# The FFN norm's sums of squares: from columns of the transposed block to rows of the residual

## Chip, cores and metric

The kernel runs on one core of one Trainium2 chip. The metric is the device time of one execution in microseconds (us), as the median of several runs. The core has a matrix engine (TensorE, PE in the profile; its weight loads are PEld), VectorE (DVE), ScalarE (ACT), GpSimd (POOL) and SyncE (SP), each with its own in-order instruction stream; they meet at semaphores.

## The reference

Two transformer-like layers run one after the other on 256 tokens of width D = 2048, in float32. What matters here lies in the middle of the first:

```
h = h + nsa_mixer(rmsnorm(h, mix_norm_g), ...)        # attention, its last product is "out"
h = h + swiglu(rmsnorm(h, ffn_norm_g), ffn_w_in, ffn_w_out)
rmsnorm(x, g) = x * rsqrt(mean(x*x, axis=-1) + 1e-6) * g
```

The FFN norm needs, for each of the 256 tokens, the sum of the squares of the 2048 features of h. The factor rsqrt(...) of a token is not applied to the operand of the product with ffn_w_in, but to the product's rows afterwards.

## The kernel before

Every large product is computed in three partial products of split float32 numbers (high times high, high times low, low times high). Weights stream through a ring of four slots in chunks of 128x1024: SP loads a chunk into `raw` (L402), ACT rounds it to the high part `w_hl` (`split`, L531), DVE subtracts to get the low part (L890), and TensorE uses it in 12 products of 128x512 (L1591 to L1593 in `block_tokens`), one chunk's work. ACT and DVE prepare a chunk three chunks ahead of TensorE (`AHEAD = 3`): ACT may write the slot of chunk c as soon as TensorE has finished chunk c-4. Work that is not splitting is put by hand between the splits: a table such as `{2: out_operand(3), ...}` says what follows the split of step j, for ACT, DVE and TensorE separately.

The attention's output product has four blocks of 512 features (B_OUT to B_OUT+3). For block n

- DVE adds the product to the residual, `row_block(n)` of `h_rows`, which has tokens in partitions: two pieces of 128 tokens x 512 features (`out_block`, L1195). This raises `taken`.
- TensorE transposes the block into PSUM, `by_features`, with features in partitions (`out_by_features`, eight transposes at L1863).
- ACT makes the high operand times the gain (L554), DVE the low one (L920), which raises `x_ready`.
- ACT squares the transposed block, 128x1024, into `sq` (`out_square`, L570), which raises `sq_ready`.
- DVE adds the 1024 columns down to 256 and onto `stat` (`h_squares`, which is `add_squares`, L956 to L961), which raises `stats_ready`.

Block 3 is handled inside the first block of the up product, `up(0, True)`. Its eight chunks are numbered 0 to 7 here, and 8 to 15 are those of the value half that follows. TensorE's steps there are: after chunk 1 the transposes of block 3, after chunk 4 the call `stats(0, 2, 5)`. That waits for DVE's last addition and multiplies `stat` by ones: two 128x256 instructions (L1696) that give the sums along a row and repeat them in all partitions, and four one-column instructions (L1698) that give them once for each partition's token. DVE makes the mean plus epsilon and its reciprocal from the 258 columns (`variance`, L926 and L927), ACT takes the root (`root`, L564), and the columns `S:S+2` of `rms[:, FFN]` scale the rows of the up product in the Sigmoid (L697) and on DVE (L1237, L1243). The 256 columns in front of them are not read in the FFN.

`down_squares` and `final_squares` do the same by columns for the final norm, with `sq` again.

Of the kernel before, what the change touches and what calls it, by code (L numbers as in the profile page):

```python
# [10 lines left out]
ACT = mybir.ActivationFunctionType  # L11
# [140 lines left out]
def program(nc, d):  # L152
    ctx = ExitStack()

    def sb(name, shape, dt=F32, scope=ctx):
        return scope.enter_context(nc.sbuf_tensor(name, shape, dt))

    def sem(name):
        return ctx.enter_context(nc.semaphore(name))
# [12 lines left out]
    cross = sb("cross", [P, HT, S])  # L172
    rms = sb("rms", [P, 4, S + TT])
    rtmp = sb("rtmp", [P, S + TT])


    with ExitStack() as s1:
# [119 lines left out]
    dve_own, act_own, pool_own = sem("dve_own"), sem("act_own"), sem("pool_own")  # L297
    xh_ready, x_ready = sem("xh_ready"), sem("x_ready")
    sq_ready, stats_ready, stats_sum = sem("sq_ready"), sem("stats_ready"), sem("stats_sum")
    var_ready, rms_ready = sem("var_ready"), sem("rms_ready")  # L300
    rel_done, u_ready, u_out, bias_in = sem("rel_done"), sem("u_ready"), sem("u_out"), sem("bias_in")
    gates_sig, gates_done, gates_ready = sem("gates_sig"), sem("gates_done"), sem("gates_ready")
# [216 lines left out]
    def _(act):  # L519
# [20 lines left out]
        def splits(at, count, extras=None, unit=None, the_set=0):  # L540

            for j in range(count):
                split(at, j + AHEAD)
                if unit is not None and j == count // 2:
                    take_cross(at.at(j), unit, sums(the_set)[1], cross[:, :, :])
                if extras and j in extras:
                    extras[j]()
            if unit is not None:
                take_cross(at.at(count), unit + 1, sums(the_set + 1)[1], cross[:, :, :])
# [9 lines left out]
            for f in range(FT):  # L559
                operand(bass.ds(n * FT + f, 1), gain, by_features[:, f:f + 1, :])  # L560

        def root(n, count):
            act.wait_ge(var_ready, count)
            a(rms[:, n, :], rtmp[:, :], ACT.Sqrt).then_inc(rms_ready, 1)  # L564

        def square(dst, src, free, scale=1.0):

            if free is not None:
                act.wait_ge(stats_ready, free)
            return a(dst, src, ACT.Square, scale=scale)  # L570
# [99 lines left out]
        def out_operand(n):  # L670
            block_operand(n, FFN, n + 1)

        def out_square(n):

            act.wait_ge(x_ready, KT + FT * (n + 1))
            square(sq[:, :, :], by_features, n + 1).then_inc(sq_ready, 1)

        splits(Pos(C_OUT), 2 * NB, attentions(3, ATT_SLOTS + 1))
        splits(Pos(C_OUT + 2 * NB), NB, {0: lambda: out_operand(0), 2: lambda: out_square(0), 4: lambda: out_operand(1),
                                         6: lambda: out_square(1)})  # L680
        splits(Pos(C_OUT + 3 * NB), NB, {2: lambda: out_operand(2), 4: lambda: out_square(2)})

        def up_high(i):
            act.wait_ge(ft_done, i + 1)
# [1 line left out]

        def up(i, first):
            at = Pos(C_UP, i, 2 * NB)
            splits(at, NB, {2: lambda: out_operand(3), 3: lambda: out_square(3), 6: lambda: root(FFN, 2)} if first else
                   {2: lambda: up_high(i - 1)})  # L690
            act.wait_ge(chunks_done, at.at(NB))

            act.wait_ge(taken, i * 2 + B_UP)
            if first:
                act.wait_ge(rms_ready, 2)
            for t in range(TT):
                last = a(f_a[:, t, :], up_set(0)[:, t, :], ACT.Sigmoid, scale=col(FFN, t))  # L697
            last.then_inc(up_sig, 1)
            splits(Pos(C_UP + NB, i, 2 * NB), NB)
# [7 lines left out]

        def down_squares(n):
            act.wait_ge(x_ready, 2 * KT + FT * (n + 1))
            square(sq[:, :, :], by_features, 5 + 2 * n).then_inc(sq_ready, 1)  # L710
            for f in range(FT):
                kt = n * FT + f
                last = square(f_squares[:, f, :], by_features[:, f, :], None, gains[:, FINAL, kt:kt + 1])
            last.then_inc(sq_ready, 1)
# [164 lines left out]
    def _(dve):  # L879
# [330 lines left out]
            dve.wait_ge(chunks_done, C_OUT + 14)  # L1210
            out_block(0)

        def h_squares(n):
            return lambda: add_squares(sq, 0, n + 5, n == 0)

        splits(Pos(C_OUT), 2 * NB, heads_out(3, ATT_SLOTS + 1) | {14: first_out}, softmaxes(3, ATT_SLOTS))
        out_block(1)
        splits(Pos(C_OUT + 2 * NB), NB, {1: lambda: out_operands(0), 3: h_squares(0), 5: lambda: out_operands(1), 7: h_squares(1)})
        out_block(2)
        splits(Pos(C_OUT + 3 * NB), NB, {3: lambda: out_operands(2), 5: h_squares(2)})  # L1220
        out_block(3)

        def up_low(i):
# [2 lines left out]
            tt(f_hl[:, kts, 1, :], by_features, f_hl[:, kts, 0, :].bitcast(F32), ALU.subtract).then_inc(f_ready, 1)  # L1226

        def up(i, first):
            splits(Pos(C_UP, i, 2 * NB), NB, {2: lambda: out_operands(3), 4: h_squares(3), 5: lambda: variance(2, 2)} if first else
                   {3: lambda: up_low(i - 1)})  # L1230
            if first:
                dve.wait_ge(rms_ready, 2)

            def gated():
                dve.wait_ge(up_sig, i + 1)
                for t in range(TT):
                    last = stt(f_a[:, t, :], up_set(0)[:, t, :], col(FFN, t), f_a[:, t, :], ALU.mult, ALU.mult)  # L1237
                last.then_inc(taken, 1)

            splits(Pos(C_UP + NB, i, 2 * NB), NB, {1: gated})  # L1240
            dve.wait_ge(taken, i * 2 + (B_UP + 1))
            for t in range(TT):
                last = stt(f_b[:, t, :], up_set(1)[:, t, :], col(FFN, t), f_a[:, t, :], ALU.mult, ALU.mult)  # L1243
            last.then_inc(taken, 1)
# [6 lines left out]
            block_operands(n, None, 2 * KT + n * FT)  # L1251

        def final_squares(j, first):
            return {first: lambda: add_squares(sq, 0, 9 + 2 * j, j == 0),
                    first + 1: lambda: add_squares(f_squares, 1, 10 + 2 * j, j == 0)}

        for n in range(4):
            splits(Pos(C_DOWN + n * ND), ND, {3: lambda n=n: down_operands(n - 1)} | final_squares(n - 1, 5) if n else
# [32 lines left out]
        def mlstm(i, first):  # L1291
# [4 lines left out]
            no_cross = NO_CROSS_ML + 3 * i  # L1296

            if first:
                splits(at, NB, {1: lambda: down_operands(3)} | final_squares(3, 3) | {6: lambda: variance(4, 2), 7: second_variance}, half=lambda: summed(
                    t1[:, 0:2, :], number, the_set, NO_CROSS_ML).then_inc(taken, 1))  # L1300

                summed(t1[:, 2:4, :], number + 1, the_set + 1, NO_CROSS_ML).then_inc(taken, 1)
                dve.wait_ge(taken, number + 2)
                dve.wait_ge(rms_ready, 4)
                own.link(tt(rms[:, PRE, :], rms[:, PRE, :], rms[:, FINAL, :], ALU.mult))
                tt(t1[:, :, :], t1[:, :, :], rows(PRE), ALU.mult).then_inc(first_normed, 1)
                splits(Pos(C_ML + NB), 1)
                dve.wait_ge(crossed, B_ML + 3 - NO_CROSS_ML)
                own.link(tt(g_fm[:, :], sets[(B_ML + 2) % 2][0:2 * MH, 0:S], cross[0:2 * MH, 0, :], ALU.add))
                tt(g_fm[:, :], sets[(B_ML + 2) % 2][0:2 * MH, S:2 * S], g_fm[:, :], ALU.add).then_inc(taken, 1)  # L1310
                dve.wait_ge(taken, B_ML + 3)
                tt(g_fm[:, :], g_fm[:, :], rms[0:2 * MH, PRE, 0:S], ALU.mult).then_inc(gates_normed, 1)
            else:

                splits(at, NB, {0: lambda: z_silu_tokens(i - 1), 1: lambda: ya_product(i - 1), 4: lambda: ya_low(i - 1)},
                       half=lambda: take(number, the_set, no_cross, t1[:, 0:2, :], PRE))
                take(number + 1, the_set + 1, no_cross, t1[:, 2:4, :], PRE)
# [253 lines left out]
    def _(pe):  # L1571
# [299 lines left out]
        def out_by_features(n):  # L1871
            if n == 0:
                pe.wait_ge(o_ready, HEADS)
            else:
                pe.wait_ge(x_ready, KT + FT * n)
                pe.wait_ge(sq_ready, 4 + n)
            rows_by_features(B_OUT + n, n)

        out_by_features(0)
# [5 lines left out]
        def up_by_features(i):  # L1885

            pe.wait_ge(taken, i * 2 + (B_UP + 2))
            if isinstance(i, int) and i == 0:
                pe.wait_ge(x_ready, 2 * KT)
                pe.wait_ge(sq_ready, 8)  # L1890
            else:
                pe.wait_ge(f_ready, i)
            back_by_features(f_b, ft_done)

        def up(i, first):
            await_set(i * 2 + B_UP)
            gemm_tokens(Pos(C_UP, i, 2 * NB), B_UP, ready=operand_ready(KT) if first else None,
                        steps={1: lambda: out_by_features(3), 4: lambda: stats(0, 2, 5)} if first else {1: lambda: up_by_features(i - 1)})
            await_set(i * 2 + (B_UP + 1))
            gemm_tokens(Pos(C_UP + NB, i, 2 * NB), B_UP + 1)  # L1900

# [3 lines left out]
        def down_by_features(n):  # L1905
            if n == 0:
                pe.wait_ge(f_ready, NUP)
            else:
                pe.wait_ge(x_ready, 2 * KT + FT * n)
                pe.wait_ge(sq_ready, 8 + 2 * n)  # L1910
            rows_by_features(B_DOWN + n, 4 + n)

        for n in range(4):
# [12 lines left out]
        def mlstm(i, first):  # L1926
            at, number = ml_block(i, 0)

            def norms():
                stats(0, 2, 13)  # L1930
                stats(1, 3, 13)


            gemm(at, number, ml_set(i, 0), ready=operand_ready(2 * KT) if first else None,
# [284 lines left out]
```

## Time and profile before

| | |
|---|---|
| runs | 2116.81, 2116.83, 2116.71 us, median 2116.81 |
| span of the profiled execution, first to last instruction | 2115.2 us |
| TensorE busy | 2104.1 us (99%); its weight loads 1772.3 us (84%) |
| DVE, ACT, POOL busy | 60%, 48%, 3% |
| idle time of TensorE with a named releaser | 1.5, 1.3 and 1.2 us |
| granted TensorE clock | 0.999 |

The page gives the profiled execution's span and no other time for it; the runs' median is 1.6 us above that span, which is what lies around the instructions. Busy time of TensorE counts overlapping instructions: a product is shown as 0.39 us long while the next starts 0.23 us after it, so its pace is read from starts, not from durations.

### The profile page before, as it was taken

How to read it: one execution, taken by the hardware profiler on the slowest of the kernel's cores; microseconds unless marked ns; L12 is line 12 of the kernel's file. 1: busy time of each engine (PE TensorE's matmuls, PEld its weight loads, DVE VectorE, ACT ScalarE, POOL GpSimd, SP SyncE). 2: the span in 40 equal slices, each digit the busy share in tenths (PEclk: the TensorE clock that was granted, in tenths of full speed). 3: DMA queues.
4: the chain of work that ended last, by engine and by line, in shares of the span. 5: the costliest groups of instructions: out<-in, count | busy, mean ns of one | idle time of the engine just before them, and what ended most of it. 6: DMA issues, size and time to landing. Idle time of an engine off the chain costs nothing.

```text
span 2115.2 us, 29340 instructions
## 1 busy us (share of the span) xinstructions
PE 2104.1 (99%) x10154; PEld 1772.3 (84%) x10154; DVE 1274.7 (60%) x1725; ACT 1010.9 (48%) x1330; POOL 64.1 (3%) x117
## 2 busy tenths in 40 slices
PE   9999999999999999999999999999999999999998
PEld 8888888888888888888888888888888888888887
DVE  7767665655555555545556766856857655455464
ACT  6465665454444444434444555444454454444444
POOL 1001221000000000000000000000000000000000
PEclk9999999999999999999999999999999999999999
DMA  8586334555555555555555455555555556555564
GB/s 299 187 275 227 139 131 144 185 179 190 190 192 184 190 190 191 188 192 189 189 189 193 157 179 178 189 177 185 189 175 183 176 184 195 190 189 191 195 229 149
DMA packets 109386, 398.72 MB, mean 189 GB/s; under 512 B 12437, under 2 KB 12469, under 8 KB 108915
## 3 DMA queue, kind: packets, MB, share of 16 engines
q1 hardware_dynamic: 106848, 386.97, 54.2%
q0 software_dynamic: 2304, 10.51, 1.4%
q8 instruction: 60, 0.98, 0.2%
q14 instruction: 30, 0.22, 0.0%
q10 hardware_dynamic: 144, 0.03, 0.0%
HBM read 393.00 MB, written 2.13 MB: 187 GB/s over the span
## 4 chain that ended last, share of the span: by engine, by line
PE 99%; ACT 0%; DVE 0%; DMA 0%; POOL 0%; issue 0%; DVEq 0%; SPq 0%; ACTq 0%
PE set L1593 23%; PE set L1591 23%; PE set L1592 23%; PE set L1617 13%; PE set L1625 7%; PE misc L1863 1%; PE misc L1744 1%; PE set L1715 1%; PE misc L1817 1%; PE misc L1804 1%; PE misc L1996 0%; PE set L1719 0%; PE misc L1790 0%; PE set L1675 0%; PE misc L1956 0%; PE misc L1792 0%
## 5 line engine op out<-in xcount | busy, mean ns | idle before, releaser
L890 DVE TENSOR_TENSOR w_hl<-raw,w_hl 128x1024 fp32r<-128x1024 f32 x729 | 890.8, 1224 | 745.0 <-ACT w_hl L531 743.0
L531 ACT ACTIVATE w_hl<-raw 128x1024 fp32r<-128x1024 f32 x729 | 771.0, 1059 | 970.6 <-PE set L1593 792.7
L1591 PE MATMUL set<-w_hl,x_hl 128*128 128x512 f32 x1408 | 553.5, 393 | 0.0
L1593 PE MATMUL set<-w_hl,x_hl 128*128 128x512 f32 x1408 | 548.6, 390 | 0.0
L1592 PE MATMUL set<-w_hl,x_hl 128*128 128x512 f32 x1408 | 547.9, 389 | 0.0
L1593 PEld LDWEIGHTS set<-w_hl,x_hl 128*128 128x128 f32 x1408 | 264.3, 188 | 55.5
L1592 PEld LDWEIGHTS set<-w_hl,x_hl 128*128 128x128 f32 x1408 | 264.5, 188 | 54.4
L1591 PEld LDWEIGHTS set<-w_hl,x_hl 128*128 128x128 f32 x1408 | 264.4, 188 | 54.1
L1617 PE MATMUL set<-x_hl,w_hl 128*128 128x512 f32 x1216 | 296.2, 392 | 0.0
L1617 PEld LDWEIGHTS set<-x_hl,w_hl 128*128 128x128 f32 x1216 | 222.2, 188 | 43.2 <-issue 0.7
L1625 PE MATMUL set<-x_hl,w_hl 128*128 128x256 f32 x1216 | 163.5, 284 | 0.0
L1625 PEld LDWEIGHTS set<-x_hl,w_hl 128*128 128x128 f32 x1216 | 157.4, 191 | 6.9 <-issue 0.7
L1591 PE MATMUL set<-w_hl,f_hl 128*128 128x512 f32 x352 | 137.3, 390 | 0.0
L1593 PE MATMUL set<-w_hl,f_hl 128*128 128x512 f32 x352 | 137.0, 389 | 0.0
L1592 PE MATMUL set<-w_hl,f_hl 128*128 128x512 f32 x352 | 136.9, 389 | 0.0
L1593 PEld LDWEIGHTS set<-w_hl,f_hl 128*128 128x128 f32 x352 | 66.1, 188 | 13.8
L1592 PEld LDWEIGHTS set<-w_hl,f_hl 128*128 128x128 f32 x352 | 66.1, 188 | 13.6
L1591 PEld LDWEIGHTS set<-w_hl,f_hl 128*128 128x128 f32 x352 | 66.1, 188 | 13.6
L1591 PE MATMUL set<-w_hl,o_hl 128*128 128x512 f32 x128 | 51.0, 399 | 0.0
L1593 PE MATMUL set<-w_hl,o_hl 128*128 128x512 f32 x128 | 50.0, 391 | 0.0
L1592 PE MATMUL set<-w_hl,o_hl 128*128 128x512 f32 x128 | 49.9, 390 | 0.0
L1591 PE MATMUL set<-w_hl,ya_hl 128*128 128x512 f32 x128 | 49.8, 389 | 0.0
(319 smaller groups left out, 1741.2 us busy)
## 6 DMA issues: line engine op xcount, KB each, us to landing
raw<-in_weights SPq DMA_DIRECT2D x730, 512.0 KB, 3.3
bias_g<-bias POOLq DMA_DIRECT2D x4, 572.0 KB, 3.4
h<-in_x SPq DMA_DIRECT2D x4, 512.0 KB, 7.0
bias<-u_dram POOLq DMA_DIRECT2D x1, 2048.0 KB, 13.6
h<-in_x_rows POOLq DMA_DIRECT2D x1, 2048.0 KB, 10.2
out<-y_t SPq DMA_DIRECT2D x8, 256.0 KB, 2.0
cur<-in_cur POOLq DMA_DIRECT2D x4, 285.0 KB, 3.7
gain_row<-in_final POOLq DMA_DIRECT2D x1, 1024.0 KB, 5.8
```

Source lines behind the costliest of these rows:

```text
L531: a(high, whole, ACT.Copy).then_inc(hi_ready, 1)
L890: tt(low, whole, high.bitcast(F32), ALU.subtract).then_inc(lo_ready, 1)
L1591: mm(o, hl[:, kt, 0, x], w[:, 0, c], start=first and k == 0, stop=False, skip_group_check=True)
L1592: mm(o, hl[:, kt, 0, x], w[:, 1, c], start=False, stop=False, skip_group_check=True)
L1593: last = mm(o, hl[:, kt, 1, x], w[:, 0, c], start=False, stop=True, skip_group_check=True)
L1617: last = mm(out[:, f * 2 * S:(f + 1) * 2 * S], w[:, 0, c], hl[:, kt, :, :], start=first and k == 0, stop=low_first, skip_group_check=True)
L1625: last = mm(out[:, f * 2 * S + S:(f + 1) * 2 * S], w[:, 1, c], hl[:, kt, 0, :], start=False, stop=not low_first, skip_group_check=True)
L1715: mm(out[:, f * 2 * S:(f + 1) * 2 * S], w[:, 0, c], x_hl[:, kt, :, :], start=kt == 0, stop=False, skip_group_check=True)
L1744: last = mm(out, blk_hl[:, n, kt, :], w[:, :, k * CH:(k + 1) * CH], start=kt == 0, stop=kt == CB - 1, skip_group_check=True)
L1804: tr(m[b][:, k * P:(k + 1) * P], pr[:, o + k * P:o + (k + 1) * P], ident[:, :])
L1817: mm(m[1][:, 0:S], v_g[:, b, 0, :], prob_t[:, b, 0:S], start=b == 0, stop=False)
L1863: last = nc.tensor.transpose(by_features[:, f, t * P:(t + 1) * P], src[:, t, f * P:(f + 1) * P], ident[:, :])
```

## The change

For the FFN norm alone, ACT takes the squares of block n from the residual's rows: two instructions over 128 tokens x 512 features, each with an accumulator output that holds one sum per token. The four blocks' sums stand in `ffn_sq`, 128x2x4. DVE adds the four, makes the mean plus epsilon and the reciprocal on two columns; ACT takes the root of two columns. DVE's four `h_squares`, TensorE's `stats` call of this norm and TensorE's waits for `sq_ready` before transposes go away, and the numbers of the semaphores that the final norm uses are shifted. The squares stay at the same places of ACT's order.

```diff
+    ffn_sq = sb("ffn_sq", [P, TT, 4])
-        def root(n, count):
+        def root(n, count, cols=slice(0, S + TT)):
             act.wait_ge(var_ready, count)
-            a(rms[:, n, :], rtmp[:, :], ACT.Sqrt).then_inc(rms_ready, 1)
+            a(rms[:, n, cols], rtmp[:, cols], ACT.Sqrt).then_inc(rms_ready, 1)
...
-        def out_square(n):
-
-            act.wait_ge(x_ready, KT + FT * (n + 1))
-            square(sq[:, :, :], by_features, n + 1).then_inc(sq_ready, 1)
+        def row_squares(n):
+
+            act.wait_ge(taken, B_OUT + n + 1)
+            if n == 0:
+                act.wait_ge(stats_ready, 1)
+            else:
+                act.wait_ge(rows_squared, n)
+            for t in range(TT):
+                last = a(flat(sq[:, 2 * t:2 * t + 2, :]), row_block(n)[:, t, :], ACT.Square, accum_out=ffn_sq[:, t, n:n + 1])
+            last.then_inc(rows_squared, 1)
...
-            splits(at, NB, {2: lambda: out_operand(3), 3: lambda: out_square(3), 6: lambda: root(FFN, 2)} if first else
+            splits(at, NB, {2: lambda: out_operand(3), 3: lambda: row_squares(3), 6: lambda: root(FFN, 2, slice(S, S + TT))} if first else
...
-        def h_squares(n):
-            return lambda: add_squares(sq, 0, n + 5, n == 0)
+        def row_variance():
+            dve.wait_ge(rows_squared, 4)
+            sums = rtmp[:, S:S + TT]
+            own.link(v.tensor_reduce(sums, ffn_sq[:, :, :], mybir.AxisListType.X, ALU.add))
+            own.link(v.tensor_scalar(sums, sums, 1.0 / D, EPS, ALU.mult, ALU.add))
+            v.reciprocal(sums, sums).then_inc(var_ready, 1)
...
-            splits(Pos(C_UP, i, 2 * NB), NB, {2: lambda: out_operands(3), 4: h_squares(3), 5: lambda: variance(2, 2)} if first else
+            splits(Pos(C_UP, i, 2 * NB), NB, {2: lambda: out_operands(3), 5: row_variance} if first else
...
                 pe.wait_ge(x_ready, KT + FT * n)
-                pe.wait_ge(sq_ready, 4 + n)
...
-                        steps={1: lambda: out_by_features(3), 4: lambda: stats(0, 2, 5)} if first else {1: lambda: up_by_features(i - 1)})
+                        steps={1: lambda: out_by_features(3)} if first else {1: lambda: up_by_features(i - 1)})
```

## Rows read from the trace of the kernel before

**Rows 1.** The page: span, busy time by engine, the chain that ended last.
```profile
span 2115.2 us, 29340 instructions
PE 2104.1 (99%) x10154; PEld 1772.3 (84%) x10154; DVE 1274.7 (60%) x1725; ACT 1010.9 (48%) x1330; POOL 64.1 (3%) x117
PE 99%; ACT 0%; DVE 0%; DMA 0%; POOL 0%; issue 0%; DVEq 0%; SPq 0%; ACTq 0%
```

**Rows 2.** TensorE's waits, whole span: us in total, times, longest us.
```profile
PE misc L1804 <- POOL prob L481: 1.5, 1, 1.5
PE misc L1696 <- DVE stat L961: 1.3, 1, 1.3
```

**Rows 3.** Timeline of TensorE around the stats call: start us, us, instruction, idle before.
```profile
411.91 0.39 PE L1592 MATMUL set<-w_hl,x_hl 128*128 128x512 f32 x1
...
416.89 0.39 PE L1593 MATMUL set<-w_hl,x_hl 128*128 128x512 f32 x1
418.55 0.70 PE L1696 MATMUL misc<-stat,ones 128*128 128x256 f32 x2 [1.27 <-DVE stat L961]
419.09 0.50 PE L1698 MATMUL misc<-ones,stat 128*128 128x1 f32 x4
419.45 0.48 PE L1591 MATMUL set<-w_hl,x_hl 128*128 128x512 f32 x1
419.77 0.40 PE L1592 MATMUL set<-w_hl,x_hl 128*128 128x512 f32 x1
...
421.60 0.39 PE L1591 MATMUL set<-w_hl,x_hl 128*128 128x512 f32 x1
```

**Rows 4.** Stretches: length, busy (x instructions) by engine, clock, DMA share, GB/s.
```profile
417.00:420.00 3.00, 1.73 (x10) 1.31 (x9) 2.93 (x5) 1.06 (x1) 0.00 (x0) 1.00 0.53 187
420.00:428.00 8.00, 8.00 (x37) 6.62 (x36) 4.27 (x4) 5.11 (x6) 0.00 (x0) 1.00 0.37 131
```

**Rows 5.** Timeline of DVE, from 415 us.
```profile
415.75 1.23 DVE L890 TENSOR_TENSOR w_hl<-raw,w_hl 128x1024 fp32r<-128x1024 f32 x1 [1.49 <-ACT w_hl L531]
416.89 0.69 DVE L956 TENSOR_TENSOR sq<-sq 128x512 f32<-128x512 f32 x1
...
418.47 1.23 DVE L890 TENSOR_TENSOR w_hl<-raw,w_hl 128x1024 fp32r<-128x1024 f32 x1
...
420.09 1.77 DVE L927 RECIPROCAL rtmp<-rtmp 128x258 f32<-128x258 f32 x1
```

**Rows 6.** Timeline of ACT, the squares of blocks 0 and 3, and the Sigmoid.
```profile
364.16 1.03 ACT L570 ACTIVATE sq<-misc 128x1024 f32<-128x1024 f32 x1
365.67 1.06 ACT L531 ACTIVATE w_hl<-raw 128x1024 fp32r<-128x1024 f32 x1 [0.48 <-PE set L1593]
...
412.90 1.01 ACT L570 ACTIVATE sq<-misc 128x1024 f32<-128x1024 f32 x1
414.66 1.06 ACT L531 ACTIVATE w_hl<-raw 128x1024 fp32r<-128x1024 f32 x1 [0.75 <-PE set L1593]
...
427.92 1.27 ACT L697 ACTIVATE f_a<-set,rms 128x512 f32<-128x512 f32 x2 [0.30 <-PE set L1593]
```

**Rows 7.** Groups of ACT, shapes apart: busy us, mean ns, idle before.
```profile
L634 ACT ACTIVATE prob<-prob,ntop 128x256 f32<-128x256 f32 x32 | 15.9, 496 | 0.0
...
L745 ACT ACTIVATE t<-t 128x512 f32<-128x512 f32 x4 | 2.5, 633 | 5.2 <-DVE t L968 4.7 <-DVE t L1306 0.5
...
L847 ACT ACTIVATE sq<-set 128x512 f32<-128x512 f32 x8 | 4.7, 585 | 7.1 <-PE set L1605 7.1
...
L847 ACT ACTIVATION_READ_ACCUMULATOR sq<-set 128x1 f32 x8 | 1.5, 192 | 0.0
```

**Rows 8.** Groups of DVE, shapes apart.
```profile
L1128 DVE TENSOR_REDUCE top<-prob 128x2 f32<-128x30 f32 x16 | 2.9, 184 | 0.6
...
L1457 DVE RECIPROCAL den<-den 128x2 f32<-128x2 f32 x8 | 1.3, 166 | 0.3
```

More of the change, by code:

```diff
@@ L299, in program @@
     sq_ready, stats_ready, stats_sum = sem("sq_ready"), sem("stats_ready"), sem("stats_sum")
+    rows_squared = sem("rows_squared")
     var_ready, rms_ready = sem("var_ready"), sem("rms_ready")
@@ L671, in out_operand @@
             block_operand(n, FFN, n + 1)
-        def out_square(n):
-            act.wait_ge(x_ready, KT + FT * (n + 1))
-            square(sq[:, :, :], by_features, n + 1).then_inc(sq_ready, 1)
+        def row_squares(n):
[7 more added lines that the diff above has]
+            last.then_inc(rows_squared, 1)
         splits(Pos(C_OUT), 2 * NB, attentions(3, ATT_SLOTS + 1))
-        splits(Pos(C_OUT + 2 * NB), NB, {0: lambda: out_operand(0), 2: lambda: out_square(0), 4: lambda: out_operand(1),
-                                         6: lambda: out_square(1)})
-        splits(Pos(C_OUT + 3 * NB), NB, {2: lambda: out_operand(2), 4: lambda: out_square(2)})
+        splits(Pos(C_OUT + 2 * NB), NB, {0: lambda: out_operand(0), 2: lambda: row_squares(0), 4: lambda: out_operand(1),
+                                         6: lambda: row_squares(1)})
+        splits(Pos(C_OUT + 3 * NB), NB, {2: lambda: out_operand(2), 4: lambda: row_squares(2)})
         def up_high(i):
@@ L709, in down_squares @@
             act.wait_ge(x_ready, 2 * KT + FT * (n + 1))
-            square(sq[:, :, :], by_features, 5 + 2 * n).then_inc(sq_ready, 1)
+            if n == 0:
+                act.wait_ge(rows_squared, 4)
+            square(sq[:, :, :], by_features, 1 + 2 * n).then_inc(sq_ready, 1)
             for f in range(FT):
@@ L1211, in first_out @@
             out_block(0)
-        def h_squares(n):
-            return lambda: add_squares(sq, 0, n + 5, n == 0)
+        def row_variance():
[4 more added lines that the diff above has]
+            v.reciprocal(sums, sums).then_inc(var_ready, 1)
         splits(Pos(C_OUT), 2 * NB, heads_out(3, ATT_SLOTS + 1) | {14: first_out}, softmaxes(3, ATT_SLOTS))
         out_block(1)
-        splits(Pos(C_OUT + 2 * NB), NB, {1: lambda: out_operands(0), 3: h_squares(0), 5: lambda: out_operands(1), 7: h_squares(1)})
+        splits(Pos(C_OUT + 2 * NB), NB, {1: lambda: out_operands(0), 5: lambda: out_operands(1)})
         out_block(2)
-        splits(Pos(C_OUT + 3 * NB), NB, {3: lambda: out_operands(2), 5: h_squares(2)})
+        splits(Pos(C_OUT + 3 * NB), NB, {3: lambda: out_operands(2)})
         out_block(3)
@@ L1253, in final_squares @@
         def final_squares(j, first):
-            return {first: lambda: add_squares(sq, 0, 9 + 2 * j, j == 0),
-                    first + 1: lambda: add_squares(f_squares, 1, 10 + 2 * j, j == 0)}
+            return {first: lambda: add_squares(sq, 0, 5 + 2 * j, j == 0),
+                    first + 1: lambda: add_squares(f_squares, 1, 6 + 2 * j, j == 0)}
         for n in range(4):
@@ L1298, in mlstm @@
             if first:
-                splits(at, NB, {1: lambda: down_operands(3)} | final_squares(3, 3) | {6: lambda: variance(4, 2), 7: second_variance}, half=lambda: summed(
+                splits(at, NB, {1: lambda: down_operands(3)} | final_squares(3, 3) | {6: lambda: variance(3, 2), 7: second_variance}, half=lambda: summed(
                     t1[:, 0:2, :], number, the_set, NO_CROSS_ML).then_inc(taken, 1))
@@ L1889, in up_by_features @@
                 pe.wait_ge(x_ready, 2 * KT)
-                pe.wait_ge(sq_ready, 8)
             else:
@@ L1909, in down_by_features @@
                 pe.wait_ge(x_ready, 2 * KT + FT * n)
-                pe.wait_ge(sq_ready, 8 + 2 * n)
+                pe.wait_ge(sq_ready, 4 + 2 * n)
             rows_by_features(B_DOWN + n, 4 + n)
@@ L1929, in norms @@
             def norms():
-                stats(0, 2, 13)
-                stats(1, 3, 13)
+                stats(0, 2, 9)
+                stats(1, 3, 9)
             gemm(at, number, ml_set(i, 0), ready=operand_ready(2 * KT) if first else None,
```

## The prediction

> **What bounds the kernel now.** I read the page first. TensorE is busy for 99% of the span and the chain that ended last is 99% TensorE; DVE and ACT have 40% and 52% of the span free [rows 1]. So an edit is worth what it takes off TensorE's own stream, or what idle time of TensorE it ends; work that goes from DVE to ACT is worth nothing by itself. The second view is TensorE's list of waits. It has three entries in the whole kernel, and the second is this change's business: the ones product at L1696 stood 1.3 us for DVE's last addition onto `stat` at L961 [rows 2]. The third view is TensorE's timeline around that place [rows 3], from which I take the price. The last are the timelines of DVE and ACT at the same place [rows 5, 6] and the groups with their shapes, for the prices of what is added [rows 7, 8].
>
> **What leaves TensorE.** The call `stats(0, 2, 5)` goes: two products of 128x256, four of one column, and the wait before them. I don't sum their durations, because TensorE's instructions overlap in the record (0.70 and 0.50 us for the two groups, one starting 0.54 us after the other). I take the stretch between ordinary products instead. From 411.91 to 416.89 us the timeline has 23 starts of ordinary products, so 22 intervals in 4.98 us, 0.2264 us each [rows 3]. From the start at 416.89 us, the last before the call, to the one at 421.60 us there are ten further ordinary starts (419.45, 419.77 and eight more) in 4.71 us. Ten intervals at the ordinary pace are 2.26 us. The rest, **2.45 us**, is what the call costs. It divides into 1.27 us of recorded idle time and 1.18 us for the six instructions and the two seams around them. The second seam is visible: the interval from 419.45 to 419.77 us is 0.32 us and not 0.23.
>
> The removed waits for `sq_ready` in front of the transposes are worth nothing: no transpose (L1863) appears among the three waits of TensorE, of which rows 2 give the two longest, so none of them ended an idle time.
>
> **The clock.** The granted clock is 1.00 in the stretch that holds the stall and in the 8 us behind it [rows 4]; the array ran at the upper of its two levels (2.4 GHz) before and after it. So the stall costs its own length and no slow products behind it, and the saving is not larger than 2.45 us on that account.
>
> **What ACT does in its place.** A block's square was one instruction of 1.03 us [rows 6]. Now it is two of 128x512, each followed by a read of the accumulator. The nearest row is the kernel's own last norm, which does just this from PSUM: 585 ns and 192 ns [rows 7]. The residual lies in SBUF; the nearest SBUF-to-SBUF row of 128x512 is a Sigmoid of 633 ns. A pair is then between 2 x (585 + 192) = 1.55 us and 2 x (633 + 192) = 1.65 us. The dearest row is the softmax's, 496 ns for 256 columns; 512 columns at twice that and one read are 2 x 0.496 + 0.19 = 1.18 us, 2.4 us a pair. I keep it as the upper bound and 1.6 us as the likely value, since the last norm's row has the same function and shape. So ACT has 0.5 to 0.6 us more for each of four blocks, at most 1.4 us.
>
> What covers it? Behind the square of block 0, ACT is idle for 0.48 us until TensorE frees a slot [rows 6]; blocks 1 and 2 look the same. There the next split comes 0.0 to 0.15 us later than now, at the bound 0.9 us. For block 3 the square starts at 412.90 us and the next split was released at 414.66 us, so 1.6 us just fit. Behind a late split stand DVE's low part and then TensorE. TensorE's need is far away. The high part of chunk 7 starts at 414.66 us on ACT, its low part at 415.75 us on DVE [rows 5]; the low part of chunk 8 starts at 418.47 us and ends at 419.70 us. TensorE, without the call, starts chunk 5 at 416.89 + 0.23 = 417.12 us and a chunk takes 12 x 0.2264 = 2.72 us, so chunk 8 starts at 425.3 us. The lead is 5.6 us (before: about 8.0 us), and this is also the lead in the steady stream, where a split starts one chunk's end after the slot is freed and three chunks are in hand. ACT's extra 0.15 us, or even 0.9 us, is covered; without that cover the likely case would cost at most 3 x 0.15 us.
>
> **What leaves DVE and what it gets.** Four groups of additions go; that of block 3 takes from 416.89 us to the next instruction's start at 418.47 us, 1.58 us [rows 5], the others as much or one instruction less. So do the mean and reciprocal over 258 columns, of which the reciprocal alone is 1.77 us [rows 5]. In their place come three instructions on two columns; the nearest rows are a reduction at 184 ns and a reciprocal at 166 ns [rows 8], so some 0.55 us with the waits between. DVE is not on the chain, and this is worth nothing by itself. `row_variance` waits for ACT's fourth pair, and what is queued behind it is the low part of chunk 9. That pair ends at 412.90 + 1.6 = 414.5 us, at the bound 415.3 us; DVE comes to the wait after the low part of chunk 8, at 419.7 us. So the wait is over before it is asked, by more than 4 us.
>
> **The root and the Sigmoid.** The root of two columns instead of 258 comes at the same step, after the split of chunk 9. All of this is timed by TensorE's chunks, so it moves forward with them. The Sigmoid waited 0.30 us for TensorE and started at 427.92 us [rows 6]; with TensorE 2.45 us earlier that is 425.5 us. The product that needs its buffer next is chunk 16, at 425.3 + 8 x 2.72 = 447.0 us, more than 15 us behind the Sigmoid and DVE's reading. Nothing there can hold TensorE.
>
> **Where the saved time could be given back.** After 420 us the wait list has no entry for TensorE, and weights arrive to the same rule (a load when DVE has done with the slot). DMA is at 0.37 to 0.53 here [rows 4]. Everything behind moves 2.45 us forward as one piece, up to the tail, which starts from the last product.
>
> **The sum.** The profiled span of 2115.2 us becomes 2112.75 us. The runs' median is 1.61 us above that span and I keep that distance: 2116.81 - 2.45 = **2114.36 us**, or 0.12% less.
>
> **Rivals.**
> 1. The wait is replaced, the work is gone. If TensorE found another late partner in chunks 5 to 8, it would stand about as long as it stood for `stat`, and only the 1.18 us of instructions and seams were saved: 2115.6 us. The candidate is the low part of a chunk. For it: ACT has more to do before it and the lead shrinks from 8.0 to 5.6 us. Against it: 5.6 us is still there.
> 2. The whole gain is absorbed, 2116.8 us. TensorE would have slack in its stream that the removed instructions used, or would wait later at something that doesn't follow its pace, a load above all. For it: the weight loads are busy for only 84% [rows 1]. Against it: starts of products are 0.2264 us apart with no gap and the chain is TensorE's. The Trainium skill, in Perfetto Trace Analysis, section Identifying the Most-Contended Engine, says that matmul busy share is a bad measure and that the busy share of weight loads is the one to judge headroom by; by it TensorE would have 16% to spare. I give it little weight, since spare room between loads isn't a place into which later products can move when their starts already follow each other evenly.
> 3. Slower. ACT's row squares delay a split so far that TensorE stands for the low part of a chunk. This decides only from a pair that is more than 5.6 us longer than the old square, that is from about 6.6 us a pair against the 2.4 us of my upper bound. If a pair took 10 us, each of four blocks would cost 10 - 6.6 = 3.4 us, 13.6 us in all, less the 2.45 us: 2128 us. No row speaks for it.
> 4. More than forecast. The trace cannot show what a stall does to the products behind it beyond the ten intervals that I counted. If TensorE's other two waits also shrank (1.5 and 1.2 us), the gain would be 5.2 us, 2111.6 us. Both lie before the change in time and don't depend on it.
>
> **How the numbers follow.** The forecast has 0.84, with its own range 2113.9 to 2114.9 us (a reading error of 0.02 us at each end of the stretches, the runs' spread of 0.12 us, and some tenths for seams). Rival 1 has 0.06, rival 2 has 0.05, rival 3 has 0.03, rival 4 has 0.02. The range that I give reaches to rival 1 on the upper side and a little further than the forecast's own on the lower: 2113.5 to 2115.8 us. It leaves out rivals 2 to 4. A change of 0.2%, which is 4.2 us, is about what a measurement of this kernel can tell from no change. The forecast and rivals 1 and 2 are all within it: 0.95. Rival 4 is faster by more: 0.02. Rival 3 is slower: 0.03.
>
> **What would show it in the profile of the changed kernel.** L1696 and L1698 have six instructions fewer around 418 us, and the list of TensorE's waits has two entries, not three. Between the product that ends chunk 4 and the one that starts chunk 5 there are 0.23 us. ACT's pairs take 1.5 to 1.7 us with their reads. Products are at 0.2264 us up to the Sigmoid, and the span is 2112.6 to 2112.9 us. I'd be wrong if a wait for `w_hl` appears at TensorE between 417 and 430 us (rival 1 or 3), or if the product that stood at 421.60 us comes 2.45 us earlier and the end does not (rival 2).

## The result, and the profile after

The changed kernel takes 2128.46 us (median of 5 runs, 2128.15 to 2128.89) against 2116.81 us before: a ratio of 1.0055, 95% interval 1.0044 to 1.0066. It is 11.65 us slower where 2.45 us less was forecast. The forecast's own place came out as described, and the loss lies elsewhere. I go through the profile in that order.

The page of the changed kernel, to be held against [rows 1]; line numbers are some 14 higher on TensorE:

```profile
span 2126.7 us, 29330 instructions
PE 2117.8 (100%) x10148; PEld 1771.6 (83%) x10148; DVE 1268.7 (60%) x1715; ACT 1011.2 (48%) x1342; POOL 63.0 (3%) x117
PE 99%; ACT 0%; DMA 0%; POOL 0%; DVE 0%; issue 0%; DVEq 0%; SPq 0%
```

TensorE has six instructions fewer and is busy for 13.7 us longer. Its list of waits answers to [rows 2]:

```profile
PE misc L1699 <- DVE ones L939: 1.2, 1, 1.2
PE misc L1818 <- POOL prob L483: 0.4, 1, 0.4
PE set L1729 <- ACT w_hl L589: 0.2, 1, 0.2
```

So the wait for `stat` is gone and the one for POOL is 1.1 us shorter. The third entry, 0.2 us at L1729, was not in the list of before; it stands in front of the kernel's first large product, at 6.87 us, and that product started at 6.82 us before, so it costs nothing here. Nothing took the place of the wait for `stat`. TensorE's timeline at the seam of chunks 4 and 5, where the call stood [rows 3]:

```profile
417.69 0.39 PE L1607 MATMUL set<-w_hl,x_hl 128*128 128x512 f32 x1
417.92 0.39 PE L1605 MATMUL set<-w_hl,x_hl 128*128 128x512 f32 x1
418.14 0.39 PE L1606 MATMUL set<-w_hl,x_hl 128*128 128x512 f32 x1
```

There are 0.23 us between the products. ACT at block 3, and the Sigmoid [rows 6]:

```profile
413.70 0.62 ACT L683 ACTIVATE sq<-h 128x512 f32<-128x512 f32 x1
414.22 0.18 ACT L683 ACTIVATION_READ_ACCUMULATOR sq<-h 128x1 f32 x1
414.31 0.62 ACT L683 ACTIVATE sq<-h 128x512 f32<-128x512 f32 x1
414.83 0.19 ACT L683 ACTIVATION_READ_ACCUMULATOR sq<-h 128x1 f32 x1
415.45 1.06 ACT L533 ACTIVATE w_hl<-raw 128x1024 fp32r<-128x1024 f32 x1 [0.43 <-PE set L1607]
...
426.27 1.27 ACT L705 ACTIVATE f_a<-set,rms 128x512 f32<-128x512 f32 x2 [0.30 <-PE set L1607]
```

A pair takes 1.32 us, from 413.70 to 415.02 us, and ACT still waits for TensorE behind it. DVE's three small instructions:

```profile
420.41 0.15 DVE L1226 TENSOR_REDUCE rtmp<-ffn_sq 128x2 f32<-128x8 f32 x1
420.60 0.17 DVE L1227 TENSOR_SCALAR rtmp<-rtmp 128x2 f32<-128x2 f32 x1
420.80 0.17 DVE L1228 RECIPROCAL rtmp<-rtmp 128x2 f32<-128x2 f32 x1
```

The first product of chunk 2, before and after:

```profile
408.83 0.47 PE L1591 MATMUL set<-w_hl,x_hl 128*128 128x512 f32 x1
```

```profile
409.66 0.48 PE L1605 MATMUL set<-w_hl,x_hl 128*128 128x512 f32 x1
```

From it to the Sigmoid there were 427.92 - 408.83 = 19.09 us before; now it is 426.27 - 409.66 = 16.61 us, 2.48 us less.

Where did the time go, then? It shows in the groups of products, which are far from the edited lines. In `set<-w_hl,f_hl` w_hl is the moving operand, 512 columns, and f_hl the stationary one, 128x128, which the weight load brings. Mean duration in ns is the number behind the busy time, first in the changed kernel:

```profile
L1605 PE MATMUL set<-w_hl,x_hl 128*128 128x512 f32 x1408 | 553.4, 393 | 0.0
L1607 PE MATMUL set<-w_hl,x_hl 128*128 128x512 f32 x1408 | 548.4, 389 | 0.0
...
L1605 PE MATMUL set<-w_hl,f_hl 128*128 128x512 f32 x352 | 139.5, 396 | 0.0
L1606 PE MATMUL set<-w_hl,f_hl 128*128 128x512 f32 x352 | 139.2, 395 | 0.0
L1607 PE MATMUL set<-w_hl,f_hl 128*128 128x512 f32 x352 | 139.2, 395 | 0.0
...
L1607 PE MATMUL set<-w_hl,ya_hl 128*128 128x512 f32 x128 | 50.6, 396 | 0.0
```

and in the kernel before:

```profile
L1591 PE MATMUL set<-w_hl,f_hl 128*128 128x512 f32 x352 | 137.3, 390 | 0.0
...
L1593 PE MATMUL set<-w_hl,ya_hl 128*128 128x512 f32 x128 | 49.8, 389 | 0.0
```

Products whose stationary operand is x_hl are as before. Those with f_hl and ya_hl, and also yb_hl and m_hl, take 395 or 396 ns and took 389 or 390 before; those with o_hl take 395 to 404 and took 390 to 399. The starts say it better, since products overlap. The down product (f_hl) in the changed kernel:

```profile
982.04 0.40 PE L1605 MATMUL set<-w_hl,f_hl 128*128 128x512 f32 x1
982.28 0.40 PE L1606 MATMUL set<-w_hl,f_hl 128*128 128x512 f32 x1
...
985.31 0.40 PE L1607 MATMUL set<-w_hl,f_hl 128*128 128x512 f32 x1
```

That is 14 intervals in 3.27 us, 0.2336 us each, where the kernel before has 0.2267. Counted over 100 us, products that use f_hl (length, busy, instructions, clock, DMA share, GB/s), first before and then after:

```profile
1000.00:1100.00 100.00, 98.74 (x435) 1.00 0.55 189
```

```profile
1000.00:1100.00 100.00, 98.74 (x423) 1.00 0.55 182
```

435 products became 423. The granted clock is 1.00 in both, and TensorE waits for nobody. What these five tensors have in common is in no row of the trace, but in the order of allocation: all of them are allocated behind `ffn_sq`, and x_hl and w_hl ahead of it. `ffn_sq` takes 32 bytes of each partition of SBUF, the memory that the operands are read from. In the built programs the byte addresses in a partition are

```
            before    after    before, less w_hl0 (32896)
x_hl         65664    65664     32768 = 128 x 256
f_hl, ya_hl 129664   129696     96768 = 378 x 256
yb_hl       162432   162464    129536 = 506 x 256
m_hl        178816   178848    145920 = 570 x 256
o_hl        179584   179616    146688 = 573 x 256
```

The ring's slots of w_hl are 8192 bytes apart and all slices that a product reads start at multiples of 512 bytes within their tensor. So before the change, stationary and moving operand of every such product were a multiple of 256 bytes apart; after it, they are 32 off.

### The profile page after: what moved, and what is told of

The parts are those of the page before. It is cut to its first block, busy times and chain, and to the rows that moved or that the text cites. A ratio compares the mean times of both kernels' runs of the same rounds, so it can differ in the third digit from the quotient of the medians.

```text
span 2126.7 us, 29330 instructions
## 1 busy us (share of the span) xinstructions
PE 2117.8 (100%) x10148; PEld 1771.6 (83%) x10148; DVE 1268.7 (60%) x1715; ACT 1011.2 (48%) x1342; POOL 63.0 (3%) x117
## 4 chain that ended last, share of the span: by engine, by line
PE 99%; ACT 0%; DMA 0%; POOL 0%; DVE 0%; issue 0%; DVEq 0%; SPq 0%
PE set L1605 24%; PE set L1607 24%; PE set L1606 24%; PE set L1631 13%; PE set L1639 7%; PE misc L1877 1%; PE misc L1758 1%; PE set L1729 1%; PE misc L1831 1%; PE misc L1818 1%; PE misc L2008 0%; PE set L1733 0%; PE misc L1804 0%; PE set L1689 0%; PE misc L1968 0%; PE misc L1806 0%
## 5 line engine op out<-in xcount | busy, mean ns | idle before, releaser
L1605 PE MATMUL set<-w_hl,f_hl 128*128 128x512 f32 x352 | 139.5, 396 | 0.0
L1606 PE MATMUL set<-w_hl,f_hl 128*128 128x512 f32 x352 | 139.2, 395 | 0.0
L1607 PE MATMUL set<-w_hl,f_hl 128*128 128x512 f32 x352 | 139.2, 395 | 0.0
L1605 PE MATMUL set<-w_hl,o_hl 128*128 128x512 f32 x128 | 51.7, 404 | 0.0
L1607 PE MATMUL set<-w_hl,ya_hl 128*128 128x512 f32 x128 | 50.6, 396 | 0.0
L1607 PE MATMUL set<-w_hl,o_hl 128*128 128x512 f32 x128 | 50.6, 395 | 0.0
L1606 PE MATMUL set<-w_hl,ya_hl 128*128 128x512 f32 x128 | 50.6, 395 | 0.0
```

Of the source, the lines that this page charges most:

```text
L1605: mm(o, hl[:, kt, 0, x], w[:, 0, c], start=first and k == 0, stop=False, skip_group_check=True)
L1606: mm(o, hl[:, kt, 0, x], w[:, 1, c], start=False, stop=False, skip_group_check=True)
L1607: last = mm(o, hl[:, kt, 1, x], w[:, 0, c], start=False, stop=True, skip_group_check=True)
```

## The experiments

Pace below is the mean distance between the starts of neighbouring products of one tensor and one shape, of those under 0.30 us, from the trace. Times are medians, beside 2116.85 to 2116.91 us for the kernel before on the same chips.

**1. The layout, put back by a filler.** Theory A is the place in memory; rival B is that the edit itself (row squares, the lost wait) slows the products.

```diff
     ffn_sq = sb("ffn_sq", [P, TT, 4])
+    pad = sb("pad", [P, 24])
```

> The changed kernel with a further unused tensor of 96 bytes per partition behind ffn_sq, so that everything allocated behind them lies 128 bytes further than before the change and not 32. Theory A (place in memory: the 32 bytes of ffn_sq moved o_hl, f_hl, ya_hl, yb_hl and m_hl off a 64-byte boundary, and each product that has one of them as stationary operand starts 6 to 7 ns later): products of these tensors return to starts 0.227 us apart and the time is the one first forecast, 2114.4 us. Rival B (the row squares, or the loss of the wait, make the products slower): it stays at 2128 us.

Measured: 2126.60 us, ratio 1.0047 (1.0033 to 1.0060); pace of f_hl 0.2326 us. My expectation failed: 128 bytes are not a place that is as good as 0. This alone would have spoken for rival B, so the next two decide.

**2. Nothing but bytes.** In the kernel before, a tensor that nobody uses, behind `rtmp`:

```diff
     rtmp = sb("rtmp", [P, S + TT])
+    pad = sb("pad", [P, 8])
```

> The kernel before with nothing but an unused tensor of 32 bytes per partition at the place of ffn_sq. Theory A: 2400 products of 128x512 with a moved stationary operand start about 0.2333 instead of 0.2267 us apart, 15 us in all, less about 1 us of the wait for POOL that a slower attention output hides: 2131 us. Rival B: 2116.8 us, no change.

Measured: 2130.87 us, ratio 1.0066 (1.0051 to 1.0081). This kernel has every instruction of the one before, and the same loss. The stationary group of f_hl and the waits of this run:

```profile
L1592 PE MATMUL set<-w_hl,f_hl 128*128 128x512 f32 x352 | 139.5, 396 | 0.0
```

```profile
PE misc L1697 <- DVE stat L962: 1.3, 1, 1.3
PE misc L1686 <- DVE ones L930: 1.2, 1, 1.2
PE misc L1805 <- POOL prob L482: 0.4, 1, 0.4
```

The wait for `stat` is back to 1.3 us and the wait for POOL is 0.4 us as in the changed kernel, so that one too goes with the layout and not with the edit. The pace of f_hl is 0.2333 us. 2016 products at 6.6 ns more and the 384 of o_hl at 5.4 ns more (0.2278 to 0.2332 us) are 15.4 us, less 1.1 us of POOL's wait 14.3 us; 14.0 us were measured. Rival B fell here.

With 16 columns of filler:

> The same with 64 bytes. Theory A with a boundary of 64 bytes: 2116.8 us. If the boundary that matters is 128 bytes: about 2131 us, as with 32 bytes. Rival B: 2116.8 us.

Measured: 2131.22 us, ratio 1.0068 (1.0052 to 1.0083), so no boundary of 64 bytes.

**3. Another tensor.** x_hl alone, by 32 bytes; the second filler puts what is behind it 128 bytes on.

```diff
+    pad_a = sb("pad_a", [P, 8])
     x_hl = sb("x_hl", [P, KT, 2, S], F32R)
+    pad_b = sb("pad_b", [P, 24])
```

> The kernel before with x_hl alone moved by 32 bytes (all behind it by 128). x_hl is the stationary operand of 4224 products of 128x512 by tokens and the moving one of 1216 products of 128x512, 1216 of 128x256 and some hundred others by features. Theory A, stationary operand counts: 4224 x 6.5 ns = 27 us more, 2144 us, and L1617 and L1625 keep their pace. If the moving operand counts instead: L1617 and L1625 slow down and L1591 to L1593 with x_hl do not, under 20 us more. If both: more than 2150 us. Rival B: 2116.8 us.

Measured: 2157.33 us, ratio 1.0191 (1.0176 to 1.0207), against 2144 expected. It falls where the expectation put "if both", but what is missing is mostly in its premise that 128 bytes behind x_hl cost nothing. The pace of x_hl by tokens (x_hl stationary, w_hl moving) went from 0.2270 to 0.2333 us, 4224 x 6.3 ns = 26.6 us, and that of the other five to 0.232 or 0.233, about 5.7 ns x 2400 = 13.7 us; together 40.3 us. By features the roles are the other way round, x_hl moving and w_hl stationary, and there the two shapes part. First before, then in this kernel:

```profile
L1617 PE MATMUL set<-x_hl,w_hl 128*128 128x512 f32 x1216 | 296.2, 392 | 0.0
L1625 PE MATMUL set<-x_hl,w_hl 128*128 128x256 f32 x1216 | 163.5, 284 | 0.0
```

```profile
L1593 PE MATMUL set<-w_hl,x_hl 128*128 128x512 f32 x1408 | 561.9, 399 | 0.0
...
L1619 PE MATMUL set<-x_hl,w_hl 128*128 128x512 f32 x1216 | 301.3, 396 | 0.0
L1627 PE MATMUL set<-x_hl,w_hl 128*128 128x256 f32 x1216 | 160.5, 281 | 0.0
```

The products of 512 columns became slower, from 0.2291 to 0.2333 us between starts, those of 256 columns faster, from 0.1193 to 0.1169 us. From start to start all 2592 products by features took 2.4 us more, and POOL's wait was 1.1 us shorter. The sum is then 41.6 us; 40.4 us were measured, so it is good to about a microsecond.

The distance is not the whole of it. m_hl and w_hl have the same addresses here as in experiment 1, 128 bytes apart modulo 256, and the pace of m_hl is 0.2333 us here and 0.2324 there.

**4. The edit without the bytes.** The sums go into a filler that the kernel has in front of f_hl and that nobody reads:

```diff
-    ffn_sq = sb("ffn_sq", [P, TT, 4])
...
         f_lead = sb("f_lead", [P, 32], scope=s2)
+        ffn_sq = f_lead[:, 0:4 * TT].rearrange("p (t n) -> p t n", t=TT)
```

> The changed kernel with no tensor of its own for the sums: ffn_sq is a view of the first 8 columns of f_lead, an unused filler in front of f_hl, so that every other tensor lies where it lay before the change. Theory A (the place of the stationary operands is all that cost): 2114.4 us, products of o_hl, f_hl, ya_hl, yb_hl and m_hl at starts of 0.227 us. Rival B (something in the row squares themselves makes products dearer): 2126 to 2128 us.

Measured: 2114.39 us (2114.23 to 2114.49, 11 runs), ratio 0.9988 (0.9979 to 0.9998). Pace of f_hl 0.2268 us. The down product of this kernel, 15 intervals in 3.40 us:

```profile
981.92 0.39 PE L1607 MATMUL set<-w_hl,f_hl 128*128 128x512 f32 x1
...
985.32 0.39 PE L1607 MATMUL set<-w_hl,f_hl 128*128 128x512 f32 x1
```

This is the forecast's number, and the version that beats both kernels. 2128.46 - 2114.39 = 14.1 us is what the 32 bytes cost the edit, the same as 2130.87 - 2116.91 = 14.0 us that they cost the kernel before.

**5. Place or distance?** Three kernels, all from the one before: 256 bytes behind `rtmp`; the ring w_hl alone by 128 bytes (what is behind it by 256); and w_hl with all behind it by 128.

```diff
+    pad_a = sb("pad_a", [P, 32])
     w_hl = [sb(f"w_hl{n}", [P, 2, CC], F32R) for n in range(RING)]
+    pad_b = sb("pad_b", [P, 32])
```

The third is the same without `pad_b`.

> The kernel before with an unused tensor of 256 bytes per partition at the place of ffn_sq. 32, 64 and 128 bytes all cost 10 to 14 us and all five operands lay at 128 above a multiple of 256. If the place modulo 256 counts: 2116.8 us. If any shift costs (a place modulo 512 or more, or a relation to another tensor): about 2127 to 2131 us.

> The kernel before with the weight ring w_hl alone moved by 128 bytes and everything behind it by 256. If the stationary operand's own place counts, products by tokens (w_hl moving) keep 0.227 us and those by features (w_hl stationary) may slow down, 0 to 15 us: 2117 to 2132 us. If the distance of stationary and moving operand counts modulo 256, all 6624 products by tokens slow down by 6 ns, 40 us: 2157 us or more.

> The kernel before with w_hl and everything behind it moved by 128 bytes, so that all distances among the operands are as before. If distances count: 2116.8 us. If a stationary operand's own place modulo 256 counts: all 6624 products by tokens slow down by 6 ns, 40 us, and 2157 us or more.

Measured: 2116.95 us, ratio 1.0000 (0.9991 to 1.0010) for 256 bytes; 2155.46 us, ratio 1.0182 (1.0167 to 1.0198) for w_hl alone, with 0.2325 us for x_hl and 0.2324 for f_hl, where 2157 us or more was expected if the distance counts; 2116.91 us, ratio 1.0001 (0.9991 to 1.0010) for all together. The stationary operands have the same place modulo 256 in the second kernel as in the first, and it is 38.5 us slower; they have another place in the third, and it is as fast. The moving operand w_hl has the same place in the second and the third. What counts is the distance of the two operands, modulo 256 bytes.

**6. One tensor, and the price.**

```diff
-        f_lead = sb("f_lead", [P, 32], scope=s2)
+        f_lead = sb("f_lead", [P, 40], scope=s2)
```

> The kernel before with f_hl alone (and f_a, f_b behind it) moved by 32 bytes: f_lead has 40 columns and not 32. If the price is one per product, the 1056 products with f_hl go from 0.2268 to 0.2333 us, 6.9 us in all, the others keep theirs: 2123.7 us. If the loss comes from another tensor that was moved with it in the change: 2116.8 us.

Measured: 2123.66 us, ratio 1.0031 (1.0019 to 1.0043), and only f_hl changed its pace, to 0.2333 us. 1056 x 6.5 ns was the sum beforehand.

**7. How the cost runs with the distance.** The filler of experiment 2 with 24, 48 and 56 columns.

> The same with 96 bytes. If any distance but a multiple of 256 costs: about 2131 us. If not: 2116.8 us.

> The kernel before with an unused tensor of 192 bytes at the place of ffn_sq, so the distance of the five operands to w_hl is 192 modulo 256, that is 64 below the next multiple. If any distance but a multiple of 256 costs: 2131 us, starts at 0.2333 us, as with 64 bytes. If the sign of the distance counts or a boundary of 192 bytes exists: 2116.8 us.

> The kernel before with an unused tensor of 224 bytes at the place of ffn_sq, 32 below a multiple of 256. 192 bytes cost 2.2 ns a product, 128 bytes 5.7 ns, 32 bytes 6.6 ns. If the cost falls on toward 256: about 1 ns a product, 2118 to 2119 us. If every distance off a multiple of 64 costs 6.6 ns (as 32 and 96 did): 2131 us.

Measured, with those of before in their place:

```
bytes off   f_hl pace, us   time, us
   0          0.2268        2116.9
  32          0.2333        2130.87
  64          0.2333        2131.22
  96          0.2343        2133.12
 128          0.2326        2126.60 with the edit, so about 2129.1 without
 192          0.2289        2121.92
 224          0.2333        2130.72
 256          0.2268        2116.95
```

(0.2326 us and 2126.60 us are experiment 1's; 2.46 us is the edit's gain.) The cost isn't symmetric, nor does it fall toward 256: 192 bytes cost a third of what 32 do and 224 bytes as much as 32. For 224 bytes 2118 to 2119 us was expected if the cost fell on, and 2131 us if not; it did not. The 2131 us for 192 was wrong, and 96 bytes cost 2 us more than the 2131 us put down for them. The count of f_hl products in 100 us at 192 bytes, between the two above:

```profile
1000.00:1100.00 100.00, 98.74 (x431) 1.00 0.56 185
```

**8. Whose accesses meet?** ScalarE and VectorE split 8 of 1024 columns, from the ninth chunk on (two narrow chunks excepted); TensorE does all its products. This leaves out most of the splitting.

```diff
+            if at.n != 0 or at.base + j >= 2 * RING and at.at(j) not in NARROW:
+                high, whole = high[:, 0:8], whole[:, 0:8]
             a(high, whole, ACT.Copy).then_inc(hi_ready, 1)
```

(and the same for the low part on VectorE)

> The kernel before, in which ScalarE and VectorE split only 8 of the 1024 columns of each chunk from the ninth on (the two narrow chunks excepted); TensorE's products are the same and read what the first chunks left in w_hl. It leaves out most of the splitting. If TensorE's own two readings (stationary and moving operand) set the 0.2267 us between starts, they stay, and the time is 2116 us. If the other engines' traffic on w_hl is part of it, the starts come nearer, down to 0.215 us, and the time falls by up to 70 us.

> The same with the unused tensor of 32 bytes at the place of ffn_sq. If the cost of the distance is within TensorE's own readings: products of o_hl, f_hl, ya_hl, yb_hl and m_hl at 0.2333 us, those of x_hl at 0.2267, 14 us above b_tiny. If it comes of TensorE's reading meeting the writes of ScalarE and VectorE into w_hl: no difference between the tensors, and the time of b_tiny.

Measured, one run each: 2113.20 and 2128.39 us, 15.2 us apart. The second one's page and group:

```profile
PE 2117.8 (100%) x10154; PEld 1771.9 (83%) x10154; DVE 525.1 (25%) x1725; ACT 403.2 (19%) x1330; POOL 58.0 (3%) x117
...
L1596 PE MATMUL set<-w_hl,f_hl 128*128 128x512 f32 x352 | 139.5, 396 | 0.0
```

VectorE is down from 60% to 25% and ACT from 48% to 19%, yet f_hl's pace is 0.2333 us and that of x_hl 0.2270, the same as with all their traffic. The first has 0.2268 us for f_hl; its 3.7 us less than before are mostly the two waits (1.5 and 1.3 us), which are no longer in its list. So the traffic of these two engines on w_hl has no part in it. The Trainium skill (SBUF — State Buffer, section SBUF: two separate sides) says that TensorE's port never waits for another engine; this pair of runs agrees with that, and shows that it isn't enough to make the pace independent of the layout.

**9. The two parts of 2.45 us.** In the kernel before, the call one chunk later in TensorE's order:

```diff
-                        steps={1: lambda: out_by_features(3), 4: lambda: stats(0, 2, 5)} if first else ...
+                        steps={1: lambda: out_by_features(3), 5: lambda: stats(0, 2, 5)} if first else ...
```

> The kernel before with the stats call of the FFN norm one chunk later in TensorE's order (after chunk 5, not 4), nothing else. The forecast's 2.45 us were 1.27 us of waiting and 1.18 us of instructions and seams; here only the wait should go, since VectorE's last addition ended 1.3 us before chunk 5 would end: 2115.5 us. If the wait is worth nothing by itself: 2116.8 us.

Measured: 2115.33 us (11 runs), ratio 0.9993 (0.9984 to 1.0002). The interval includes 1, so by it alone the two kernels can't be told apart. But the highest of the 11 runs, 2115.69 us, is 1.0 us below the lowest of the 23 beside them, the span is 2113.7 against 2115.2 us, and the timeline has no idle time at the call:

```profile
419.61 0.39 PE L1593 MATMUL set<-w_hl,x_hl 128*128 128x512 f32 x1
419.84 0.59 PE L1696 MATMUL misc<-stat,ones 128*128 128x256 f32 x2
420.27 0.50 PE L1698 MATMUL misc<-ones,stat 128*128 128x1 f32 x4
420.63 0.48 PE L1591 MATMUL set<-w_hl,x_hl 128*128 128x512 f32 x1
```

1.5 us of the gain was to be had by moving one line. The remaining 0.9 us, up to experiment 4's kernel, is about the work of the call: the products around it start 420.63 - 419.61 = 1.02 us apart, 0.79 us more than ordinary ones.

## Why the prediction was wrong

**Right: what leaves TensorE.** The 2.45 us came out as 2.48 us in the trace at that place and as 2.46 us in the time of the edit without its bytes (experiment 4). The division into 1.27 us of wait and 1.18 us of work was a little off: 1.5 us went with the wait (experiment 9).

**Right: what ACT and DVE do instead, and that it is hidden.** A pair of squares was put at 1.55 to 1.65 us and takes 1.32 us: the means are 616 and 186 ns, but each instruction starts about 0.1 us before the one ahead of it ends, which a sum of means cannot show. No wait for `w_hl` appeared at TensorE between 417 and 430 us; the list of waits has three entries where two were forecast, but the third is at the kernel's start. The three small instructions on DVE end 0.56 us after the first begins, as put. The Sigmoid still waits 0.30 us for TensorE.

**Wrong: "Everything behind moves 2.45 us forward as one piece."** That is the step that failed. The prediction priced the instructions and waits that the diff takes and adds, and passed over its first line, the new tensor, which it so put at nothing without a reason. Its 32 bytes shifted five stationary operands of 2400 products from a distance of 0 to one of 32 bytes modulo 256 against the moving operand, and each product then took 6.6 ns more from start to start (5.4 ns for o_hl). That is +14.1 us on the edit's -2.46 us.

**Rival 3 gave 2128 us, and the number is no merit.** It had ACT's pair at 10 us and TensorE waiting for a chunk. The pair is 1.32 us and there is no such wait. The chance of 0.03 for slower was for that mechanism; the one that decided had none.

**Rival 2** was at odds with the trace in the way that was said: removed work did shorten the time by its whole length (experiment 4). The 0.2264 us between starts, which I took for a constant of the product, are the pace of one layout.

**Rival 4** was set aside because TensorE's other two waits "lie before the change in time and don't depend on it". One of them did: the wait for POOL went from 1.5 to 0.4 us, in the filler's kernel as in the changed one. The new tensor reaches what runs ahead of the edited code too.

**What the record of before could have told.** The diff puts a tensor ahead of `o_lead`, `f_lead` and `ya_lead`, three fillers in front of exactly those operands, with nothing reading them. That is a sign in the code that places matter here. And the trace of before has one group at other distances:

```profile
L1744 PE MATMUL misc<-w_hl,blk_hl 128*124 128x512 f32 x64 | 17.5, 395 | 0.0
```

Its stationary slices are 124 float32 numbers, 496 bytes, apart, so the distance to w_hl changes by 16 bytes modulo 256 from one product to the next. The starts within its chunks are 0.224 to 0.241 us apart, 0.2318 us in the mean of 48, against 0.2267 us for f_hl. They repeat every 16 products, and with the filler of 64 bytes the same series comes four products later, to 1 ns. The group has 124 and not 128 stationary columns and takes its 512 moving ones in two pieces, so it proves nothing by itself, but it could have given a rival and a rough price: 5 ns x 2400 products, 12 us.

**What stays open.** Which of TensorE's own accesses meet is not shown, nor that it is two of them: the weight load of one product and the moving operand of another overlap in time, and that their relative place is what counts fits it, but no run took one of them away, and the loads into `raw` stayed in every run. Why 192 bytes cost a third and 224 the full price isn't explained, nor why m_hl has two paces at one distance (experiment 3). Nor is the shorter wait for POOL in the shifted kernels (0.4 for 1.5 us). It stays at 1.5 us where f_hl alone moves (experiment 6) and at 192 bytes, so it goes with o_hl's pace or place; but with the filler of 32 bytes it also ends earlier, at 337.02 and not 337.70 us, so slower products that hide it are not the whole reason.

## What to carry to other kernels

A new tensor in a list of allocations is an edit to everything behind it. Before its price is worked out from instructions, look up which operands of the bound engine move and by how much, put the new tensor last or into space that exists, and when a time moves the wrong way, compare the mean durations of groups that the edit did not touch. A run of the old kernel with a filler of the same size separates the layout from the edit in one step.

## What the runs showed of the hardware that I had not expected

For fp32r products of 128x128 by 128x512 at the full granted clock, back to back, the distance in SBUF between stationary and moving operand, modulo 256 bytes, changes the pace: 0.2268 us at 0, and 0.2289 to 0.2343 us at the six other distances tried (f_hl; m_hl once differed by 1 ns at the same distance). Both may be shifted together by 128 bytes at no cost. With the roles the other way round (w_hl stationary, x_hl moving) a shift of 32 bytes took products of 512 columns from 0.2291 to 0.2333 us and those of 256 columns from 0.1193 to 0.1169 us, so what is best for one shape is not for another. Taking away most of the writes that two other engines make to w_hl changed neither the pace at 0 nor that at 32 bytes.
